# The first block of weights multiplied unsplit, all eight transposes of x at once, and the early loads in another order

## The reference

```python
h = _rmsnorm(x, g_mix[l])          # t * rsqrt(mean(t*t) + eps) * g
z = h @ w_in[l]                    # 1024 -> x_rnn, g_rnn, q, k, v, gate_a, gate_b
x_rnn, g_rnn, q, k, v, gate_a, gate_b = jnp.split(z, SPLIT_IDX, axis=-1)
xc = _causal_conv(x_rnn, conv_w[l], conv_b[l])
hr = _rg_lru(xc, w_rg[l], b_rg[l], w_ig[l], b_ig[l], lru_lambda[l])
```

## Time and profile before

| | |
|---|---|
| median of 3 runs | 977.16 us (976.59 to 977.18) |
| profiled execution, its own time | 977.06 us |
| profiled execution, span | 975.2 us |
| TensorE busy | 961.4 us, 99% of the span |
| VectorE, ScalarE busy | 536.9 us and 479.4 us |
| DMA, mean over the span | 229 GB/s |

### The profile page before, as it was taken

How to read it: one execution, slowest core, us unless ns; L and a number is a source line. 1 busy time by engine, 2 the same in 40 slices (tenths; PEclk the granted TensorE clock), 3 DMA queues, 4 the chain that set the end, 5 groups by cost and what they waited for, 6 DMA issues and landing times.

```text
span 975.2 us, 13582 instructions
## 1 busy us (share of the span) xinstructions
PE 961.4 (99%) x5469; PEld 734.8 (75%) x5469; DVE 536.9 (55%) x853; ACT 479.4 (49%) x766; POOL 2.1 (0%) x10
## 2 busy tenths in 40 slices
PE   9999999999999999999999999999999999999996
PEld 8878887887889888898889887889874455454443
DVE  5888896775666555645577874675362112122113
ACT  5588655756444444444665856454453222222223
POOL 0000000000000000000000000000000000000000
PEclk9999999999999999999999999999999999999998
DMA  9935565424455555554554734384299999999993
GB/s 303 318 130 173 173 215 173 158 102 173 149 178 205 182 173 174 179 199 156 171 168 154 260 105 154 130 293 151 89 357 321 395 393 394 394 393 395 393 395 151
DMA packets 107268, 223.53 MB, mean 229 GB/s; under 512 B 10185, under 2 KB 15042, under 8 KB 107202
## 3 DMA queue, kind: packets, MB, share of 16 engines
q1 hardware_dynamic: 104752, 219.10, 63.6%
q10 hardware_dynamic: 2450, 3.51, 1.1%
HBM read 221.54 MB, written 1.05 MB: 228 GB/s over the span
## 4 chain that ended last, share of the span: by engine, by line
PE 96%; DVE 2%; ACT 1%; issue 1%; POOL 0%; DVEq 0%; ACTq 0%; POOLq 0%
PE pb L463 21%; PE pb L465 21%; PE pb L464 21%; PE pb L2427 12%; PE pb L2450 6%; PE pb L2402 3%; PE pb L2465 3%; PE pb L532 2%; PE pb L603 1%; PE pb L615 1%; PE pb L552 1%; PE pb L679 1%; PE pb L2376 1%; PE pb L702 1%; PE pb L710 1%; PE pb L586 1%
## 5 line engine op out<-in xcount | busy, mean ns | idle before, releaser
L1504 DVE TENSOR_TENSOR wl<-raw,wh 128x2048 fp32r<-128x2048 f32 (+2 forms) x113 | 248.7, 2209 | 97.2 <-ACT wh L963 97.0
L963 ACT ACTIVATE wh<-raw 128x2048 fp32r<-128x2048 f32 (+2 forms) x113 | 208.0, 1848 | 110.6 <-PE pb L465 103.5
L463 PE MATMUL pb<-wh,th 128*128 128x512 f32 (+2 forms) x620 | 247.7, 400 | 0.0
L465 PE MATMUL pb<-wh,tl 128*128 128x512 f32 (+2 forms) x620 | 241.5, 389 | 0.0
L464 PE MATMUL pb<-wl,th 128*128 128x512 f32 (+2 forms) x620 | 241.3, 389 | 0.0
L463 PE MATMUL pb<-th,wh 128*128 128x256 f32 x544 | 156.5, 288 | 0.2 <-DVE wl L1987 0.2
L465 PE MATMUL pb<-th,wl 128*128 128x256 f32 x544 | 153.5, 282 | 0.0
L464 PE MATMUL pb<-tl,wh 128*128 128x256 f32 x544 | 153.3, 282 | 0.0
L463 PEld LDWEIGHTS pb<-wh,th 128*128 128x128 f32 x620 | 116.7, 188 | 27.0 <-issue 4.1
L465 PEld LDWEIGHTS pb<-wh,tl 128*128 128x128 f32 x620 | 116.7, 188 | 25.4
L464 PEld LDWEIGHTS pb<-wl,th 128*128 128x128 f32 x620 | 116.9, 189 | 22.7
(11 more groups left out here) (382 smaller groups left out, 1073.1 us busy)
## 6 DMA issues: line engine op xcount, KB each, us to landing
raw<-in_w_in SPq DMA_DIRECT2D x31, 1024.0 KB, 5.2
raw<-in_w_up SPq DMA_DIRECT2D x16, 1024.0 KB, 6.2
raw<-in_w_down SPq DMA_DIRECT2D x16, 1024.0 KB, 4.8
raw<-in_w_exp_gate SPq DMA_DIRECT2D x20, 512.0 KB, 10.5
raw<-in_w_exp_up SPq DMA_DIRECT2D x20, 512.0 KB, 11.5
raw<-in_w_exp_down SPq DMA_DIRECT2D x10, 1024.0 KB, 13.9
raw<-in_w_xkv SPq DMA_DIRECT2D x8, 1024.0 KB, 5.1
mwh<-in_w_exp_gate SPq DMA_DIRECT2D x14, 512.0 KB, 12.0
```

The costliest lines, as they stand in the source:

```text
L463: PE.matmul(o, lh, rh, start=start, stop=False, skip_group_check=True)
L465: return PE.matmul(o, ll, rh, start=False, stop=stop, skip_group_check=True)
L963: ACTE.activation(hi_of(i), raw_of(i), ACT.Copy).then_inc(S["hi"], 1)
L1504: DVE.tensor_tensor(lo_of(i), raw_of(i), hi_of(i).bitcast(F), ALU.subtract).then_inc(S["lo"], 1)
```

## The change

Unit 0 is no longer split. TensorE multiplies it as plain float32 (`pe_first`, 16 matmuls) by float32 copies of the transposed chunks, which now stand in `S1`. All eight chunks of x are transposed in one go, a chunk's bank being free as soon as its copy is out; ScalarE copies the even chunks, VectorE the odd ones, and the split of x into `TH` and `TL` is made from `S1` afterwards, two chunks at a time. The counters `hi` and `lo` now start at unit 1. Unit 1 is split in two column halves. The zeros are 7 and 1 instead of 9, 3 and 2. The sums of squares write their squares to `S0`. On SP's queue units 3 and 4 stand in front of the gates' blocks, unit 5 behind them and in front of the constants; `load(4)` waits for `used` 1 (unit 0 multiplied). The load of the memory into `S1` waits for unit 0 multiplied and x split. The order of two heads in attention's values (`pe_values`) is the same in both kernels: no line of it is in the diff. The diff, cut:

```diff
 def load(i):
             elif i >= NRAW:
                 before = NUD - NRAW + m - 3 if m >= 3 else i - NRAW
-                SP.wait_ge(S["lo"], before + 1)
+                if before == 0:
+                    SP.wait_ge(S["used"], 1)
+                else:
+                    SP.wait_ge(S["lo"], before)
 def sp_main():
             load(2)
-            SP.dma_start(CT[:, 128:CN], A["const"][:, 128:CN]).then_inc(S["d_const"], 16)
             load(3)
+            load(4)
             for j, name in enumerate(("w_rg", "w_ig")):
                 ...
+            load(5)
+            SP.dma_start(CT[:, 128:CN], A["const"][:, 128:CN]).then_inc(S["d_const"], 16)
             ...
-            for i in range(NRAW, NUD):
+            for i in range(6, NUD):
+        def copied(c):
+            return (S["xt_a"], c // 2 + 1) if c % 2 == 0 else (S["xt_d"], c // 2 + 1)
+        def pe_first():
+            w = v3(RAW[0], 4, 512)
+            for c in range(4):
+                if c % 2 == 0:
+                    PE.wait_ge(S[("d_half", "raw_0")[c // 2]], 16)
+                for k in range(4):
+                    if c == 0:
+                        PE.wait_ge(*copied(k))
+                    m = PE.matmul(PB[4 + c // 2][...], w[:, k, 128 * c:128 * c + 128], chunk(S1, k),
+                                  start=(k == 0 and c % 2 == 0), stop=False, skip_group_check=True)
             m.then_inc(S["used"], 1)
 def pe_main():
             PE.wait_ge(S["zero"], 1)
-            pe_zeros(9)
-            PE.wait_ge(S["d_ident"], 16)
+            pe_zeros(7)
+            PE.wait_ge(S["d_first"], 32)
             PE.wait_ge(S["d_x"], 16)
-            pe_turn("x", v3(X, 2, D), range(4), step=8)
-            pe_zeros(3)
-            pe_turn("x", v3(X, 2, D), range(4, 8), step=8)
-            pe_zeros(2)
+            for c in range(8):
+                if c >= 4:
+                    PE.wait_ge(*copied(c - 4))
+                for t in range(2):
+                    m = PE.transpose(PB[c % 4][:, 128 * t:128 * t + 128], v3(X, 2, D)[:, t, c:1024:8], ident)
+                m.then_inc(S["turn_mm"], 1)
+            pe_zeros(1)
 def act_main():
-            act_turn("x", range(4), "g_mix", 0, free=[(S["d_gmix"], 16)])
-            (unit 0 in two halves, act_turn of chunks 4 to 7, act_hi(1), act_square of both tiles)
+            ACTE.wait_ge(S["d_first"], 32)
+            for c in (0, 2, 4, 6):
+                ACTE.wait_ge(S["turn_mm"], c + 1)
+                ACTE.activation(chunk(S1, c), PB[c % 4][:, 0:256], ACT.Copy, scale=col("g_mix", c)).then_inc(S["xt_a"], 1)
+            for c in (4, 6, 0, 2):
+                ...
+                ACTE.activation(chunk(TH[0], c, 2), chunk(S1, c, 2), ACT.Copy).then_inc(S["turn_hi"], 2)
+            act_square("x", 0, ...)
+            (unit 1 in two column halves)
+            act_square("x", 1, ...)
             for b in range(2):
                 for r in range(2):
                     act_unit("x", b, r)
                     if (b, r) == (0, 0):
-                        ACTE.wait_ge(S["square"], 2)
+                        ACTE.wait_ge(S["used"], 1)
+                        ACTE.wait_ge(S["turn_lo"], TB_["x"] + 8)
                         ACTE.dma_start(v3(S1, 2, D), A["mem_2"][0]...).then_inc(S["d_mem1"], 16)
 def dve_main():
-            dve_turn("x", range(4), "g_mix", 0)
+            DVE.wait_ge(S["d_first"], 32)
+            for c in (1, 3, 5, 7):
+                DVE.wait_ge(S["turn_mm"], c + 1)
+                DVE.tensor_scalar(chunk(S1, c), PB[c % 4][:, 0:256], col("g_mix", c), None, ALU.mult).then_inc(S["xt_d"], 1)
+            for n, c in enumerate((4, 6, 0, 2)):
+                DVE.wait_ge(S["turn_hi"], 2 * n + 2)
+                DVE.tensor_tensor(chunk(TL[0], c, 2), chunk(S1, c, 2), chunk(TH[0], c, 2).bitcast(F), ALU.subtract).then_inc(S["turn_lo"], 2)
             (the two halves of the low part: of unit 1 instead of unit 0)
-            dve_turn("x", range(4, 8), "g_mix", 0)
-            dve_lo(1)
```

More of the change, by code:

```diff
@@ L137 @@
     [f"raw_{i}" for i in (*range(NRAW), "ga", "gb", "bt", *(f"{x}{n}" for n in range(NW) for x in ("wh", "wl")))] +
-    ["d_x", "d_rows", "d_rows2", "d_gmix", "d_ident", "d_const", "d_bd", "d_bcast", "d_mem", "d_mem1", "d_pos", "d_gffn", "d_poolw", "d_p", "d_fing",
+    ["d_x", "d_rows", "d_first", "d_const", "d_bd", "d_bcast", "d_mem", "d_mem1", "d_pos", "d_gffn", "d_poolw", "d_p", "d_fing",
      "d_out", "d_out2",
-     "d_half", "hi_half", "lo_half", "zero", "hi", "lo", "used", "evict0", "evict1", "turn_mm", "turn_hi", "turn_lo", "square", "rs", "row_mm", "row", "step_d", "step_a",
+     "d_half", "hi_half", "lo_half", "xt_a", "xt_d", "zero", "hi", "lo", "used", "evict0", "evict1", "turn_mm", "turn_hi", "turn_lo", "square", "rs", "row_mm", "row", "step_d", "step_a",
      "cols_mm", "cols", "lam", "lam_abs", "lam_exp", "xr0", "mem_rs", "xc0", "xc", "gate_mm", "gate_a", "rnn_u", "rnn_m", "rnn_root", "rnn_b",
@@ L423, in sp_main @@
                 if at >= 48:
[L424 removed]
+                    SP.dma_start(S0[at:at + n, 0:128], rows_source(name)).then_inc(S["d_rows"], 16)
             load(2)
[L426 removed]
             load(3)
+            load(4)
             for j, name in enumerate(("w_rg", "w_ig")):
@@ L449, in pe_weights @@
         def pe_weights(i):
-            if i == 0:
+            if i == 1:
                 PE.wait_ge(S["lo_half"], 1)
             else:
-                PE.wait_ge(S["lo"], i + 1)
+                PE.wait_ge(S["lo"], i)
             kc, w = shape_of(i)
@@ L495, in pe_features @@
             for c in range(4):
-                if i == 0 and c == 2:
+                if i == 1 and c == 2:
                     PE.wait_ge(S["lo"], 1)
@@ L507, in pe_features, with split_x @@
                                r == 0 and k == 0 and c % 2 == 0, r == nu - 1 and k == kc - 1)
+            m.then_inc(S["used"], 1)
+        def copied(c):
+            return (S["xt_a"], c // 2 + 1) if c % 2 == 0 else (S["xt_d"], c // 2 + 1)
+        def split_x(c):
+            return S["turn_lo"], (c // 2 - 1 if c >= 4 else c // 2 + 3) * 2
+        def pe_first():
[6 more added lines that the diff above has]
+                        PE.wait_ge(*copied(k))
+                    m = PE.matmul(PB[4 + c // 2][:, (c % 2) * 256:(c % 2) * 256 + 256], w[:, k, 128 * c:128 * c + 128], chunk(S1, k),
+                                  start=(k == 0 and c % 2 == 0), stop=False, skip_group_check=True)
             m.then_inc(S["used"], 1)
@@ L726, in pe_main @@
                 for r in range(2):
-                    pe_features(("x", b), r, 2, 0, turned("x") if b == 0 else None, {2: row_x} if (b, r) == (1, 0) else ())
+                    if (b, r) == (0, 0):
+                        pe_first()
+                    else:
+                        pe_features(("x", b), r, 2, 0, split_x if (b, r) != (1, 1) else None, {2: row_x} if (b, r) == (1, 0) else ())
                 if b == 0:
-                    PE.wait_ge(S["d_rows"], 96)
-                    PE.wait_ge(S["d_rows2"], 128)
+                    PE.wait_ge(S["d_rows"], 224)
                     PE.wait_ge(S["turn_lo"], TB_["x"] + 8)
@@ L960, in act_hi @@
             ACTE.wait_ge(S[f"raw_{slot(i)}"], landed[i])
-            if i >= NW:
+            if i > NW:
                 ACTE.wait_ge(S["used"], i - NW + 1)
@@ L1119, in act_main @@
         def act_main():
-            ACTE.dma_start(CT[:, 0:128], A["const"][:, 0:128]).then_inc(S["d_ident"], 16)
-            ACTE.dma_start(PC[:, 129:137], A["g_mix"][0].rearrange("(p k) -> p k", k=8)).then_inc(S["d_gmix"], 16)
+            ACTE.dma_start(CT[:, 0:128], A["const"][:, 0:128]).then_inc(S["d_first"], 16)
+            ACTE.dma_start(PC[:, 129:137], A["g_mix"][0].rearrange("(p k) -> p k", k=8)).then_inc(S["d_first"], 16)
             ACTE.dma_start(gffn, A["ffn_norm_g_2"][0].rearrange("(p k) -> p k", k=8)).then_inc(S["d_gffn"], 16)
@@ L1131, in act_main @@
                 ACTE.dma_start(S0[at:at + n, 128:256], rows_source(name)).then_inc(S["d_rows"], 16)
-            act_turn("x", range(4), "g_mix", 0, free=[(S["d_gmix"], 16)])
-            for h, sem in ((0, "d_half"), (1, "raw_0")):
-                ACTE.wait_ge(S[sem], 16)
-                a = slice(256 * h, 256 * h + 256)
[L1136 to L1140, removed]
+            ACTE.wait_ge(S["d_first"], 32)
[3 more added lines that the diff above has]
+            for c in (4, 6, 0, 2):
+                ACTE.wait_ge(S["xt_a"], c // 2 + 1)
+                ACTE.wait_ge(S["xt_d"], c // 2 + 1)
+                ACTE.activation(chunk(TH[0], c, 2), chunk(S1, c, 2), ACT.Copy).then_inc(S["turn_hi"], 2)
+            act_square("x", 0, S0[:, D:2 * D], v3(X, 2, D)[:, 0, :])
+            ACTE.wait_ge(S["raw_1"], landed[1])
+            for h, sem in ((0, "hi_half"), (1, "hi")):
+                a = slice(256 * h, 256 * h + 256)
+                ACTE.activation(v3(WH[1], 4, 512)[:, :, a], v3(RAW[1], 4, 512)[:, :, a], ACT.Copy).then_inc(S[sem], 1)
```

(3 more changed lines are left out.)

2 lines of the change are left out of this document (1 added, 1 removed).

## The result

The changed kernel takes 975.37 us (median of 19 runs, 974.86 to 976.11) where the kernel before takes 977.00 (19 runs, 976.39 to 980.43). The ratio of the runs is 0.9982, with a 95% interval of 0.9975 to 0.9989: 1.6 us, and the forecast of 975.5 lies 0.13 from it. The profiled execution is the shortest of the runs, 974.86 with a span of 973.1, so the two profiles differ by 2.1 us, more than the medians.

What follows compares the result with a forecast made beforehand. TensorE, busy 961.4 of 975.2 us, was taken as the bound. Gains of 0.87 and 1.88 less a loss of 1.12 gave 1.63 us, so 975.5 from the median of 977.16; own range 975.0 to 976.1, overall 974.6 to 977.4.

Steps and rivals of the forecast that it cites:

- step 1: TensorE's opening: seven zeros instead of nine let the transposes stream at 6.89 instead of 7.76, gain 0.87 us.
- step 2: First transpose to first weight matmul: 2.37 us instead of 4.25 with unit 0's split out of the chain, gain 1.88.
- step 3: Unit 0 unsplit on TensorE: 48 matmuls (5.79 us) replaced by 16 float32 ones (6.91 us), loss 1.12.
- an early rise: Clock rising earlier at the start than in the profiled execution: 0.3 to 0.9 us more gain; its case had chance 0.08.
- The clock rival: Fewer zeros around the transposes drop TensorE to the lower clock, slowing unit 0's float32 records: 978.2 to 982.3 us, chance 0.09.
- Step 4: Unit 1's split on ScalarE and VectorE: ready when TensorE needs it at 16.17, with a margin of 1.2 us.
- Step 5: SP's load queue: new order needed, old would stall TensorE some 0.4 us; put at zero, at worst takes 1.6.
- The gain is absorbed on SP's queue: Unit 5 or 6, behind the gates' blocks, lands late and eats the gain: 976.3 to 977.5 us, chance 0.14.
- The transfers set the end: DMA in the experts is the bound, leaving at most some of the gain: 976.5 us, chance 0.05.

Runs made afterwards that it cites:

- order_only: The kernel before with only the loads in the new order (units 4 and 5 ahead), old start kept: 976.28 us, ratio 0.9994.
- order_old: The changed kernel with SP's old load order (constants in front of unit 3, gates' blocks in front of unit 4): 977.23 us, ratio 1.0004.
- no_zeros: The changed kernel without any opening zeros and without the one in the gap: 976.41 us, ratio 0.9995 to the kernel before.
- before_seven: The kernel before with seven opening zeros instead of nine, nothing else: 976.56 us, ratio 0.9996.
- five_ahead: The changed kernel with unit 5 loaded ahead of the gates' blocks and unit 6 ahead of the constants: 975.43 us, ratio 0.9979.
- best: The changed kernel with five_ahead's load order, g_mix on its own semaphore, chunks 4 to 7 transposed between unit 0's first matmuls, no gap zero: 975.44 us, ratio 0.9979.

## Why the prediction held

The two profiles of each kernel make the comparison fair: the second ones have the spacing's fall at 7.07 and 6.73, near the 6.68 on which the prediction's sum stands.

| term | predicted | first profiles | second profiles |
|---|---|---|---|
| step 1, first transpose | -0.87 | -1.51 | -0.99 |
| step 2, transpose to unit 0 | -1.88 | -1.67 | -1.76 |
| step 3, unit 0 | +1.12 | +1.11 | +1.11 |
| unit 1's first matmul | -1.63 | -2.07 | -1.64 |
| unit 4 | -1.63 | -2.08 | -1.65 |
| last matmul | -1.63 | -2.10 | -1.82 |

**Step 1** was right for executions in which the clock rises late, and I took one execution's phase for a property of the kernel. If it rises at 4.1, the old nine zeros end before 6.6 (order_only: 6.52) and the new start, which waits for g_mix until 6.25 to 6.6, gains nothing there. So the term is between 0 and 1.0. I had given an early rise 0.3 to 0.9 more, not less, since I thought of after alone. How often each kernel has which is open: of five profiles with the old start one was early, of eight with the new start and its zeros seven were before 6.0. TensorE does the same work in both until 4.1 us, so I know of no reason for a difference. Thirteen profiles don't exclude chance, though they strain it: with eight early ones among thirteen, the old start's five would hold one or none in 41 of 1287 cases, 3%. On the other side, eight of order_only's eleven runs took 976.08 to 976.32, like its early profiled execution (976.13) and unlike its late one (977.19), which hints that the old start is often early too. If the change did bring the rise forward, that part of the gain is in no step of the prediction.

**Step 2** came 0.1 to 0.2 short: 2.48 and 2.58 us from the first transpose to the first weight matmul, for the 2.37 worked out. The copy by VectorE, for which there was no row, is not the reason: two of them take 0.88 where I had 0.92 (7.53 to 8.45). ScalarE and VectorE of after, at the start:

```profile
6.84 0.86 ACT L1166 ACTIVATE S<-pb,PC 128x256 f32<-128x256 f32 x2 [3.18 <-PE pb L746]
7.89 0.95 ACT L1166 ACTIVATE S<-pb,PC 128x256 f32<-128x256 f32 x2 [0.20 <-PE pb L746]
...
7.08 0.88 DVE L2023 TENSOR_SCALAR S<-pb,PC 128x256 f32<-128x256 f32 x2 [7.08 <-PE pb L746]
8.14 0.93 DVE L2023 TENSOR_SCALAR S<-pb,PC 128x256 f32<-128x256 f32 x2 [0.19 <-PE pb L746]
```

The difference sits in the records behind a wait. In the stream a transpose follows its like by 0.11, but behind a wait the next one follows by 0.21: in the first profile at the first transpose (6.25, then 6.46; it waited for g_mix) and at chunk 4 (7.36, then 7.58; it waits for a copy), in the second at chunk 4 alone. That is 0.2 and 0.1.

**Step 3** was right to 0.01: 32 records 0.216 apart ((15.52 - 8.83) / 31, first to last), real weights like zeros. The clock rival fell: with one zero product left in the gap, nothing slowed. After a longer stop the clock did fall, in order_old. The rule of the Trainium skill (TensorE: Matmul & The Clock Gate, "Part 4: PE-mode transpose"), by which the prediction took this rival to hold, is not borne out in after: 2.3 us of transposes stand ahead of unit 0 and unit 0 runs at full rate. In no_zeros the transposes came first, at half rate, and the change came 1.1 us into unit 0's matmuls, where the thirteen other profiles had 3.0 us or more of zero products before it (1.10 to 4.14 at the least). If transposes counted for nothing it should have come later, so this speaks against the rule too, but in one execution.

**Step 4** was right: no wait at unit 1, whose low part's second half VectorE ended at 15.5 (16.1 worked out).

**Step 5** is the one that failed, in its size. I said that the old order "would have stalled TensorE by some 0.4 us" and worked it out from one profile's landing of unit 4, 1.2 us ahead of its use. order_old lost 1.9 us. Two things were missing: the five broadcasts between the gates' blocks and unit 4 (5.2 us of issue in before, 8.1 in order_old), which I never counted, and that issue and landing together spread over 2 us (low part ready at 34.67 to 36.74) where the margin was 1.2; in the second profile of before it was only 0.7. With the low part ready at 35.37 or 35.99 and TensorE asking for it at 34.3, the wait would be 1.1 to 1.7 us and not 0.4, most of the 1.9; in the profiled execution the clock's fall came on top. It did not change the forecast because the forecast was for the new order, in which both go behind unit 5, and there "it can give nothing beyond the sum" held: the second profiles have the shift of unit 1 (1.64) at unit 4 (1.65). In after unit 4 landed at 26.3, for 24 worked out, and its low part was ready at 32.15, 1.7 ahead of its use. What stands behind it was faster than worked out: the gates' blocks took 5.4 us to issue (16.34 to 21.8) for 9.85, and unit 5's low part was ready at 35.3 for 39. But for executions with an early rise it gave more than nothing: with the old order such a start would wait at unit 4, as before_seven did with its transposes at 7.02, and the new order takes that wait away. There the order would give what step 1 does not. The two errors have opposite signs, and that 1.63 was forecast and 1.63 measured is in part luck. That before waits in its early executions is argued, not shown: no profile of it with an early rise came up.

**The rivals.** "The gain is absorbed on SP's queue" had the mechanism, a load behind small transfers, but for the wrong kernel and unit: it is what happens to unit 4 without the new order. "The transfers set the end" was refused too quickly: they don't in after, but the profiled executions of five_ahead and best met them at 953 us. The windows of the end in after show how near they are (before's share at 953 to 956 was 1.02, since all of it lies 2 us later there):

```profile
950.00:953.00 3.00, 3.00 (x16) 1.00 (x14) 0.90 (x2) 0.38 (x1) 0.00 (x0) 1.00 1.03 411
953.00:956.00 3.00, 3.00 (x16) 1.65 (x13) 1.38 (x2) 2.04 (x4) 0.00 (x0) 1.00 0.60 239
```

The transfers run at full share until 953 and then run out; in five_ahead a landing about there was 0.3 too late.

## What to carry to other kernels

When the first engine to start is to start earlier, ask for each of the next units when its data is due, and count everything that is queued ahead of its load: here the whole new start was worth nothing with the old order (order_old), the order of loads 0 to 0.6 alone, and both 1.6. A margin read from one profile is a sample: where it is behind a queue of small transfers, take a second profile, or make the margin larger than the spread before counting on it. And a gain in such a chain has a next limit close behind it (here VectorE's lead of 0.6 us and the last experts' transfers), so a second step of the same kind may give nothing, as five_ahead and best did.

## What the runs showed of the hardware

- TensorE's float32 records of 256 columns go from 0.43 us apart to 0.216 at some time between 4.1 and 7.2 us if it works from 1.1 us on, and for the same program that time differs from execution to execution (4.24 and 6.73; 4.14 and 7.16). If its first work is at 6.5, the change comes at 11.1. The printed granted clock is 1.00 in all these stretches, so only the spacing shows the half rate.
- In order_old TensorE started nothing from 33.89 to 36.80 us, and the granted clock was 0.50 from there to 39.6, with records of 512 columns 0.43 us apart for 0.23: 1.4 us lost on top of the wait. In before_seven, with a wait of 0.72, the records are 0.22 to 0.24 apart again from 36.38 on.
- Issuing a small DMA can hold SP for microseconds: the broadcast of q_gain, 256 bytes for each partition, took 2.59 us to issue in before and 3.98 in order_old, but 0.43 in after, where it stands later in the queue; that of the router's group bias took 0.43 in before and 0.73 in order_old. Which of the transfers under way set this is not shown.
